# Output projection by seven half-size products, sample normalised first; block scores in column groups

## The reference

```
y  = einsum('bte,ed->btd', h, w_out)            # 2048 -> 1024
xp = layer_norm(ALPHA * xp + yp, ln_g, ln_b)    # rows of 1024
```

## Time and profile before

| | |
|---|---|
| median of 3 runs | 1994.38 us (1990.13 to 1995.8) |
| the profiled execution's own time | 1991.48 us |
| its span, first to last instruction | 1989.6 us |
| mean granted clock of TensorE | 0.981 |
| busy: PE, DVE, ACT, POOL | 95%, 54%, 39%, 20% |

### The profile page before, as it was taken

The page is one execution under the profiler, slowest core; times in us unless marked ns, Lnnn a source line. Parts: engine busy times, 40 slices in busy tenths (PEclk is TensorE's granted clock), DMA queues, the critical chain, the costliest instruction groups (busy, mean ns, idle before and its releaser), DMA issues. The chain is left out here.

```text
span 1989.6 us, 45884 instructions
## 1 busy us (share of the span) xinstructions
PE 1898.0 (95%) x18746; PEld 1399.2 (70%) x18746; DVE 1077.8 (54%) x2679; ACT 768.1 (39%) x1635; POOL 391.7 (20%) x424
## 2 busy tenths in 40 slices
PE   7999999999998999999798989899999999999998
PEld 6888888866666777787466634577777777777543
DVE  3111131137885344443677324489898998888432
ACT  0000001147874443343367501145555555555300
POOL 5442323335662000000444010000000000000000
PEclk9999999999998999999799999999999999999999
DMA  6243312326137999998466499799999999993230
GB/s 182 83 153 89 91 46 91 69 75 185 52 131 189 389 384 375 382 390 343 183 243 220 149 278 322 236 320 310 354 323 313 344 310 336 330 318 97 86 118 25
DMA packets 222095, 443.36 MB, mean 223 GB/s; under 512 B 60832, under 2 KB 182192, under 8 KB 205248
## 3 DMA queue, kind: packets, MB, share of 16 engines
q1 hardware_dynamic: 214432, 364.57, 56.6%
q0 software_dynamic: 7456, 75.86, 10.5%
HBM read 413.70 MB, written 165.23 MB: 291 GB/s over the span
## 5 line engine op out<-in xcount | busy, mean ns | idle before, releaser
L2326 PE MATMUL three<-x1T,arena 128*128 128x288 f32 x768 | 201.5, 409 | 1.4 <-PEq L973 0.9
L2326 PEld LDWEIGHTS three<-x1T,arena 128*128 128x128 f32 x768 | 145.6, 191 | 41.3 <-issue 1.3
L2639 POOL TENSOR_TENSOR rec_v_own<-rec_sV,row_own 64x512 f32<-64x512 f32 x16 | 23.8, 1485 | 674.3 <-ACT rec_sV L2571 674.3
L580 POOL TENSOR_TENSOR late<-late 128x512 f32<-128x512 f32 (+2 forms) x76 | 112.1, 1476 | 219.4 <-PE pab_bZ L368 128.5
L852 ACT ACTIVATE ap_sc<-ap_sc,ap_nmax 128x256 f32<-128x256 f32 (+1 forms) x192 | 106.3, 557 | 5.0 <-DVE ap_nmax L876 4.9
L1477 DVE COPY sa_kT<-sa_bT 128x512 f32<-128x512 f32 x80 | 55.2, 690 | 93.9 <-PE sa_bT L1333 93.8
L876 DVE CUSTOM_DVE_ANT_0 ap_sc<-ap_bS,ap_bias 128x256 f32<-128x256 f32 (+1 forms) x192 | 86.1, 486 | 14.0 <-DMA ap_bias<-in_bias_p 9.5
L911 POOL TENSOR_SCALAR ap_sc<-ap_sc,ap_rden,sgl 128x256 f32<-128x256 f32 (+3 forms) x128 | 76.4, 607 | 40.4 <-DVE ap_rden L884 40.2
L1477 ACT COPY sa_kT<-sa_bT 128x512 f32<-128x512 f32 x80 | 46.9, 586 | 96.8 <-PE sa_bT L1333 96.6
L1496 DVE COPY sa_xT<-sa_bT 128x512 f32<-128x512 f32 x64 | 43.8, 684 | 67.7 <-PE sa_bT L1398 67.3
L453 ACT COPY zs<-pab_bZ 128x128 f32<-128x128 f32 (+2 forms) x22 | 6.4, 290 | 173.9 <-PE pab_bZ L368 173.9
(11 more groups left out here) (522 smaller groups left out, 4473.6 us busy)
## 6 DMA issues: line engine op xcount, KB each, us to landing
out<-in_cache_a_k SPq DMA_DIRECT2D x8, 8160.0 KB, 28.9
out<-in_cache_a_v SPq DMA_DIRECT2D x8, 8160.0 KB, 29.6
arena<-in_cache_a_k SPq DMA_DIRECT2D x40, 1024.0 KB, 8.7
arena<-in_cache_a_v SPq DMA_DIRECT2D x40, 1024.0 KB, 9.5
arena<-in_w_in_c SPq DMA_DIRECT2D x64, 512.0 KB, 6.9
late<-in_w_in_ab SPq DMA_DIRECT2D x128, 64.0 KB, 2.3
late<-in_w_in_ab SPq DMA_DIRECT2D x8, 1024.0 KB, 5.2
ap_bias<-in_bias_p SPq DMA_DIRECT2D x16, 512.0 KB, 3.9
```

The source lines that it names most:

```text
L580: nc.gpsimd.tensor_tensor(to, a, b, op).then_inc(sums, 1)
L2326: last = nc.tensor.matmul(grouped(bank[:, 0:NT_HALF]), left[:, k, :], right[:, k, :, :], start=(first and k == 0), stop=(k == 3), skip_gro ...
L2639: nc.gpsimd.tensor_tensor(v_own[:, :, :], sV[0:TS, :].unsqueeze(1).broadcast_to([TS, HALF_NB, P]), row_own[:, :].unsqueeze(2).broadcast_to ...
```

## The change

**Block scores.** The block keys become the stationary operand (32 columns) and the queries of one r over all 512 tokens the moving one. Four values of r go to the four groups of 32 partitions of one bank. ScalarE copies the two banks to `by_head` in SBUF; TensorE transposes them back in eight pieces behind product 4 (`turn_scores`), and VectorE adds the mask in eight instructions behind its add of product 5, each later step one place further on.

**Output projection.** The 512 tokens by 2048 channels and 2048 channels by 1024 columns are cut in halves each way: A11 is tiles 0 and 1 with slabs 0 to 7, A12 the same tiles with slabs 8 to 15, A21 and A22 tiles 2 and 3; B11 is row blocks 0 to 7, left 512 columns, and so on. Seven products of such halves stand for eight; a product is 2 tiles by 8 slabs, 16 matmuls. A11 x B11 and the sample's slabs 0 to 7 are now the work that is laid into and behind the last head. VectorE forms four sums of A and four of B, the latter and three of the former in place, and adds the banks to the rows of x in SBUF as they come. The sample is normalised first. `Norm.vector` is cut in two (`moments`) so that the prompt's tiles can use its second part; `merge` issues the same instructions as before.

Of the diff, the declarations of buffers and semaphores and the lines of `Norm` are left out; code is moved to the left.

```diff
+    for j in range(2):
+        for c in range(4):
+            last = nc.tensor.matmul(bC[j][32 * c:32 * c + 32, :], kc_p[:, :], qT[1][:, 4 * j + c, :], start=True, stop=True,
+                                    skip_group_check=True)
+        last.then_inc(s_done, 1)
+def turn_scores():
     for m in range(TILES):
-        into = bC[m // 2][:, 256 * (m % 2):256 * (m % 2) + 256].rearrange("p (g r n) -> p g r n", g=KVB, n=PBLK)
-        for r in range(RB):
-            last = nc.tensor.matmul(into[:, :, r, :], qT[1][:, r, m * P:(m + 1) * P],
-                                    kc_p[:, :].rearrange("p (g n) -> p g n", g=KVB), start=True, stop=True)
+        pe.wait_ge(s_copied, 2)
+        for j in range(2):
+            at = 256 * (m % 2) + P * j
+            last = nc.tensor.transpose(bC[m // 2][:, at:at + P], by_head[:, j, m * P:(m + 1) * P], ident[:, :])
         if m % 2 == 1:
-            last.then_inc(s_done, 1)
+            last.then_inc(s_turned, 1)
...
+if (u, i) == (10, 4):
+    turn_scores()
...
+if u == 10:
+    for j in range(2):
+        act.wait_ge(s_done, j + 1)
+        nc.scalar.copy(by_head[:, j, :], bC[j][:, :]).then_inc(s_copied, 1)
...
-if (u, i) == (10, 2):
-    for j in range(2):
-        dve.wait_ge(s_done, j + 1)
-        two = slice(2 * j, 2 * j + 2)
-        line(nc.vector.tensor_tensor(sc[:, two, :, :], bC[j][:, :].rearrange("p (m h n) -> p m h n", m=2, n=PBLK),
-                                     off[:, two, :].unsqueeze(2).broadcast_to([P, 2, HB, PBLK]), ALU.add))
 if (u, i) == (10, 3):
+    for m in range(TILES):
+        dve.wait_ge(s_turned, m // 2 + 1)
+        for g in range(KVB):
+            line(nc.vector.tensor_tensor(
+                sc[:, m, RB * g:RB * g + RB, :],
+                bC[m // 2][:, 256 * (m % 2):256 * (m % 2) + 256].rearrange("p (r g n) -> p g r n", g=KVB, n=PBLK)[:, g, :, :],
+                off[:, m, :].unsqueeze(1).broadcast_to([P, RB, PBLK]), ALU.add))
+if (u, i) == (10, 4):
     line(nc.vector.tensor_reduce(mx[:, :, :], sc[:, :, :, :], AX_X, ALU.max))
-if (u, i) == (10, 4):
+if (u, i) == (10, 5):
     nc.vector.tensor_tensor(scf, scf, mxf.unsqueeze(2).broadcast_to(flat), ALU.subtract).then_inc(exp_in, 1)
...
-                def project_ahead(k):
+                def first_product(k):
                     if k in (0, 4, 7):
                         n = (0, 4, 7).index(k)
                         pe.wait_ge(next_in[n], (64, 48, 64)[n])
-                    for n, (m, half) in enumerate(OUT_AHEAD):
-                        nc.tensor.matmul(bR[n][:, :], oT[:, k, m * P:(m + 1) * P], next_rows[k][:, 512 * half:512 * half + 512],
+                    for t in range(2):
+                        nc.tensor.matmul(bR[t][:, :], oT[:, k, t * P:(t + 1) * P], next_rows[k][:, 0:512],
+                                         start=(k == 0), stop=(k == OUT_HALF - 1), skip_group_check=True)
+                def sample_rows(k):
+                    for half in range(2):
+                        nc.tensor.matmul(bR[2][TS * half:TS * half + TS, :], oT[:, k, SEQ:TOK], next_rows[k][:, 512 * half:512 * half + 512],
                                          start=(k == 0), stop=False, skip_group_check=True)
                 for h in range(HC + 1):
@@ -2514,19 +2542,24 @@
                     else:
                         pe.wait_ge(added, ADDS * HC)
                         pe.wait_ge(out_ready, len(next_rows))
-                        project_ahead(0)
+                        for k in (0, 1):
+                            first_product(k)
                         turn_values(h - 1)
                         pairs(h - 1)
-                        project_ahead(1)
+                        for k in (2, 3):
+                            first_product(k)
                         updates(h - 1)
-                        project_ahead(2)
+                        for k in (4, 5):
+                            first_product(k)
                         outputs(h - 1)
                         own_outputs(h - 1)
-                        project_ahead(3)
+                        first_product(6)
                     if behind:
                         squares(h - 1)
-                for k in range(4, len(next_rows)):
-                    project_ahead(k)
+                for k in range(7):
+                    sample_rows(k)
+                first_product(7)
+                sample_rows(7)
...
-ORDER = (0, 1, TILES, 2, 3)
...
+ORDER = (TILES, 0, 1, 2, 3)
+LEFT, RIGHT = slice(0, 512), slice(512, 1024)
+def heads(late, half):
+    return oT[:, OUT_HALF * late:OUT_HALF * late + OUT_HALF, 2 * P * half:2 * P * half + 2 * P]
+A11, A12, A21, A22 = heads(0, 0), heads(1, 0), heads(0, 1), heads(1, 1)
+def rows(late, c):
+    return [w[OUT_HALF * late + k][:, c] for k in range(OUT_HALF)]
+B11, B12, B21, B22 = rows(0, LEFT), rows(0, RIGHT), rows(1, LEFT), rows(1, RIGHT)
+S2, S3, S4 = A11, A21, A12
+T1, T2, T3, T4 = B11, B11, B12, B21
...
-def project(m, k, halves=(0, 1)):
-    for half in halves:
-        last = nc.tensor.matmul(acc[m % 2][half][:, :], oT[:, k, m * P:(m + 1) * P], w[k][:, 512 * half:512 * half + 512],
-                                start=(k == 0), stop=(k == 15), skip_group_check=True)
-        if k == 15:
-            last.then_inc(y_done, 1)
-def project_sample(k):
+def product(left, right, bank, t, first, arriving=False):
+    for k in range(OUT_HALF):
+        if arriving and OUT_HALF + k >= AHEAD:
+            pe.wait_ge(w_in[OUT_HALF + k], 16)
+        last = nc.tensor.matmul(bank[:, :], left[:, k, t * P:(t + 1) * P], right[k], start=(first and k == 0),
+                                stop=(k == OUT_HALF - 1), skip_group_check=True)
+    return last
+for t in range(2):
+    pe.wait_ge(first_copied, t + 1)
+    product(A12, B21, acc_a[t], t, False, True).then_inc(c11_done, 1)
+for k in range(OUT_HALF, 16):
     for half in range(2):
         last = nc.tensor.matmul(acc_s[n * half:n * half + n, :], oT[:, k, SEQ:TOK], w[k][:, 512 * half:512 * half + 512],
-                                start=(k == 0), stop=(k == 15), skip_group_check=True)
-    return last
-for k in range(AHEAD):
-    project(1, k, (1,))
-for k in range(AHEAD):
-    project_sample(k)
-for k in range(AHEAD, 16):
-    pe.wait_ge(w_in[k], 16)
-    for m in range(2):
-        project(m, k)
-for k in range(AHEAD, 16):
-    last = project_sample(k)
+                                start=False, stop=(k == 15), skip_group_check=True)
 last.then_inc(ys_done, 1)
-pe.wait_ge(normed, 1)
-for k in range(16):
-    project(2, k)
-pe.wait_ge(normed, 2)
-for half in range(2):
-    for k in range(16):
-        project(3, k, (half,))
+pe.wait_ge(s1_ready, 1)
+pe.wait_ge(t1_ready, 1)
+for t in range(2):
+    product(S1, T1, acc_b[t], t, True).then_inc(p5_done, 1)
+pe.wait_ge(s4_ready, 1)
+for t in range(2):
+    pe.wait_ge(p5_read, t + 1)
+    product(S4, B22, acc_b[t], t, False).then_inc(c12_done, 1)
+pe.wait_ge(s2_ready, 1)
+pe.wait_ge(t2_ready, 1)
+for t in range(2):
+    product(S2, T2, acc_d[t], t, True).then_inc(p6_done, 1)
+pe.wait_ge(s3_ready, 1)
+pe.wait_ge(t3_ready, 1)
+for t in range(2):
+    pe.wait_ge(p6_read, t + 1)
+    product(S3, T3, acc_d[t], t, False).then_inc(p7_done, 1)
+pe.wait_ge(t4_ready, 1)
+for t in range(2):
+    pe.wait_ge(p7_read, t + 1)
+    product(A22, T4, acc_d[t], t, False).then_inc(p4_done, 1)
...
+for t in range(2):
+    nc.scalar.copy(first[t][:, :], acc_a[t][:, :]).then_inc(first_copied, 1)
+act.wait_ge(ys_done, 1)
+nc.scalar.copy(y2[:, :], acc_s[n:P, :]).then_inc(y2_ready, 1)
...
+def token_sum(to, a, b, op):
+    return nc.vector.tensor_tensor(to, a, b, op)
...
+def weight_sum(to, a, b, arriving=False):
+    for k in range(OUT_HALF):
+        if arriving and OUT_HALF + k >= AHEAD:
+            dve.wait_ge(w_in[OUT_HALF + k], 16)
+        last = nc.vector.tensor_tensor(to[k], a[k], b[k], ALU.subtract)
+    return last
+def add(to, a, b):
+    return nc.vector.tensor_tensor(to, a, b, ALU.add)
+def normalize(i, m, r, stats, parts):
+    norm.moments(dve, line, i, P, r, stats)
+    for half in range(parts):
+        c = slice(D_MODEL // parts * half, D_MODEL // parts * (half + 1))
+        norm.scaled(P, x1[:, m, :], c, r).then_inc(normed, 1)
+    dve.wait_ge(normed, i + parts)
+token_sum(S1[:, :, :], A21, A22, ALU.add).then_inc(s1_ready, 1)
+weight_sum(T1, B12, B11).then_inc(t1_ready, 1)
+dve.wait_ge(s1_ready, 1)
...
+token_sum(S3, A11, A21, ALU.subtract).then_inc(s3_ready, 1)
+dve.wait_ge(s3_ready, 1)
+token_sum(S2, S1[:, :, :], A11, ALU.subtract).then_inc(s2_ready, 1)
+dve.wait_ge(s2_ready, 1)
+dve.wait_ge(c11_done, 2)
+token_sum(S4, A12, S2, ALU.subtract).then_inc(s4_ready, 1)
+dve.wait_ge(x_in, 16 * TILES)
+dve.wait_ge(first_copied, 2)
+for t in range(2):
+    for m, c in ((t, RIGHT), (t + 2, LEFT), (t + 2, RIGHT)):
+        last = nc.vector.scalar_tensor_tensor(out=x1[:, m, c], in0=x1[:, m, c], scalar=ALPHA, in1=first[t][:, :],
+                                              op0=ALU.mult, op1=ALU.add)
```

(52 more changed lines are left out.)

35 lines of the change are left out of this document (23 added, 12 removed).

## The result

The changed kernel takes 1979.44 us (median of 4 runs, 1978.39 to 1979.92), the kernel before 1994.49 beside it (1990.13 to 1995.8). The ratio is 0.9925 with a 95% interval of 0.9904 to 0.9945. The forecast was 1975.5, with a range of 1970 to 1984.5. In a later set, with more runs, the same kernel took 1977.15 against 1996.01. The two differences of medians, 15.1 and 18.9 us, stand for the forecast 18.9.

A forecast was written before the change was run, and what follows sets the result against it. TensorE alone was taken to bound the output projection. Block scores -7.5, fillers -8.2 and output block -3.2 sum to -18.9 us: profiled 1991.48 to 1972.6, plus 2.9 for the median, 1975.5; range 1970 to 1984.5.

The forecast's parts named there:

- Block scores: First projection, unit 10: new scores replace 10.46 us by matmuls, transposes and small seams; -7.5 us, bounds -8.0 and -2.4.
- two column groups' price holds for four: New block scores: eight matmuls in four column groups run side by side as two do in the sample rows; 1.74 us.
- the transposes: First projection: eight transposes turn the new scores back, taken at 1.0 us from the same eight elsewhere.
- The first rival: Block scores: the 32-column groups take turns, 6.87 us for 1.74, giving 1980.6 us; chance 8%.
- Fillers: Last head: 9 x 0.859 = 7.7 us less product work before the barrier and a filled 0.49 us wait; -8.2 us.
- Output block: Final output projection: TensorE ends 93.1 us after the block's start, before 96.3; -3.2 us.
- the late weights: Output block, tile 0: last weight rows land at 9.4 us, a new TensorE wait of 2.7 us, bounds 0 and 5.
- the two waits: Start of the output block: ScalarE's copy (0.7 us) and weights' arrival (2.7 us) take back 3.4 us.
- The third rival: Output block: VectorE becomes the bound at 1.32 us a sum, giving 1984.5 us; chance 6%.
- The second rival: The granted clock falls to half in the new waits, costing 3.3 us and giving 1978.8 us; chance 13%.
- The stages between 300 and 1848: Stages between the two edited places, in us of the timeline; their growth would show the prediction wrong.
- the fourth rival: The first projection's 7.5 us are not handed down, as a later stage is paced by transfers; 1983.0 us, chance 9%.

The follow-up runs named there:

- out_only: The kernel before with only the new output projection and the old block scores; median 1982.87 us, ratio 0.9934.
- pad: The changed kernel with 79 more long-satisfied semaphore waits in TensorE's instructions ahead of the block scores; one run, 1977.31 us.
- sample_first: The changed kernel with three of the sample's row blocks ahead of the output block's late products, which go row by row, and five behind; 1978.27 us, ratio 0.9903.
- slow_sums: The changed kernel with an unused VectorE subtraction of 128x512 ahead of every weight sum of the output block; 1980.72 us, ratio 0.9929.
- before_again: The kernel before, unchanged, run once more for a second trace; one run, 1995.82 us.
- after_again: The changed kernel, unchanged, run once more in a later set; 1977.15 us, ratio 0.9909 against the kernel before.
- best: The changed kernel with the sample's rows moved ahead of the output block's late products and a GpSimd wait in the selected blocks; 1974.34 us, ratio 0.9893.

## Why the prediction was right

**Block scores.** Forecast -7.5, measured -7.6 in every trace. The step that two column groups' price holds for four (1.74) was right at 1.86; the transposes took 0.9 us as the earlier trace rows said, and the clock held. The first rival, groups in turns, would have had 175.4 in this stretch and is out.

**Fillers.** Forecast -8.2, measured -7.9 without the gap (out_only, pad) and -5.7 with it. The arithmetic of 9 products at 0.859 was right. What was missing is that TensorE's instructions have to be fetched, and that shifting the stream can lay a fetch where nothing covers it.

**Output block.** Forecast -3.2, measured -2.8 and, in the second trace, -3.1. TensorE's first product started 0.65 us after the block's start for 0.7. The last row block landed at 9.6 for 9.4 (9.2 in the second trace), tile 1 began at 10.6 for 10.3, and the late weights cost 3.1 for 2.7 (from the starts; the 1.65 of the list of waits is less than they cost). That is most of the 0.4 by which the block ended later than the forecast 93.1. That sample_first gains 3.1 to 3.4 bears out the 3.4 that I had put down for the two waits.

**VectorE.** It kept pace, as forecast. The third rival (9 us lost at 1.32 us a sum) did not come, as the sums took 0.686; at 1.2 us a sum VectorE cost 0.2.

**The clock.** The second rival did not come in the changed kernel's trace: its longest wait in the block was 1.32 us. The chance of 13% was not idle, though. With a wait of 1.74 at the same place the clock did fall (slow_sums), for some 1.3 us of the 3.3 put down for it, and in runs whose traces were not taken it may have.

**Handing down.** The stages between 300 and 1848, whose growth the prediction named as a sign of being wrong, did grow in this pair of traces, by 3.6 us. In the second pair (before_again and after_again) they shrank by 1.8. Of the fourth rival's kind is a part in `merge`, which the prediction took to move with its stage: TensorE waited 8.4 and 8.7 us there for `mab_hT` in the two traces of the changed kernel, 5.7 and 5.1 in those of the kernel before, and the stage took 142.5 and 143.1 us against 140.8 and 138.3. It is no fixed limit, since the three kernels with GpSimd's wait start the recurrence 9 to 13 us ahead of the first trace of before, and best, with 139.1 us in `merge`, is the earliest. What holds these transfers up is open. The larger part was a block of VectorE behind GpSimd, of up to 4 us, and a spread of 3.6 us that two traces of the kernel before have between them. Whether the change itself lengthens the stretch by a microsecond or two is open.

**The sum.** The profile moved by 13.1 and the medians by 15.1 and 18.9. The forecast on the median stood within 4 us of both results, and the terms that missed it in the first pair (2.5 in the last head, 0.4 in the block, some 3 upstream) all lie on one side. In the second pair the spans differ by 19.1 us: 10.2 up to the first filler, 5.7 in the last head, 3.1 in the block. That the 18.9 was met there is luck in part, since the last head's 2.5 too little stand beside 2.7 too much upstream.

## What to carry to other kernels

A row of small matmuls costs twice, by itself and by the clock that it takes from what follows: cut it into pieces among long products (3.3 us here) or lay its stationary operands in column groups (7.6 us). Before a gain is costed at its full size, look at what lies where it arrives (VectorE operations with two inputs in SBUF beside a row of GpSimd's, a hundred tiny instructions in a microsecond), and take two traces of the kernel before, since its stretches differ by more than a small edit is worth. Where weights must first arrive, begin the block with the work whose operands are there and let the late ones go row by row: 3 us here for no arithmetic at all.

## What the runs showed of the hardware

Four matmuls with 32 stationary and 512 moving columns in the four column groups of one bank took 0.93 us, against 0.859 for one full one.

A VectorE multiplication of 128x128 with both inputs in SBUF took 0.29 us alone and 4.0 to 5.2 beside GpSimd's additions of 1.03 us, which themselves did not slow down; it did not get in between them in seven traces, and in three, where GpSimd's row had begun 4.4 us ahead of it, it did (0.76 and 0.77).

TensorE stood still for 1.74 to 2.39 us with nothing to wait for, beside a fetched block of 16 KB of instructions, and adding 40 instructions 580 us earlier moved the place by 38. Of the 65 gaps of over 1 us of this kind in 13 traces, 64 end 1.2 to 1.7 us behind the end of such a packet. Behind gaps of 1.80, 2.35 and 2.39 us in the last head the granted clock fell to half, behind those of 1.74 to 1.78 in five traces it did not; but behind a wait of 1.74 for weights it fell as well, and behind gaps of 1.98 and 2.25 elsewhere it stayed at 1.00.
